# Two of eight final row tiles normalised by GpSimd and ScalarE in place of VectorE, in a hybrid encoder layer with a mixture of experts

## What is computed

```python
def expert_choice_moe(h, router_w, w_gate, w_up, w_down):      # tok: 512 tokens of one sequence
    gate, idx = lax.top_k(aff.T, cap)                           # cap = 64
    xs = tok[idx]
    hid = silu(xs @ w_gate) * (xs @ w_up)
    ye = (hid @ w_down) * gate[..., None]
    out = zeros_like(tok).at[idx].add(ye)

x = x + expert_choice_moe(rmsnorm(x, norm2_g), ...)
return rmsnorm(x, norm_f_g)                                     # the final norm, factor norm_f_g
```

## Time and profile before

| what | value |
|---|---|
| median of 3 runs | 1541.17 us |
| the profiled execution, its own time | 1543.18 us |
| its span, first to last instruction | 1541.4 us |
| mean granted TensorE clock | 0.977 of full |
| TensorE busy | 1464.4 us (95%) |
| VectorE busy | 1186.8 us (77%) |
| ScalarE busy | 816.1 us (53%) |
| GpSimd busy | 163.8 us (11%) |

### The profile page before, as it was taken

One profiled execution on the slowest core, in us unless ns is written; L12 is line 12 of the kernel. 1 busy time (PEld: TensorE's weight loads), 2 busy tenths in 40 slices (PEclk: granted clock), 3 DMA queues, 4 the chain that ended last, 5 costly groups with the idle time before them and its releaser, 6 DMA issues.

```text
span 1541.4 us, 18595 instructions
## 1 busy us (share of the span) xinstructions
PE 1464.4 (95%) x6886; PEld 1225.6 (80%) x6886; DVE 1186.8 (77%) x1002; ACT 816.1 (53%) x760; POOL 163.8 (11%) x121
## 2 busy tenths in 40 slices
PE   7999999999989999996499999999999999999994
PEld 6878888877768888785388888888888888888883
DVE  5688888985647766324698888888988888889887
ACT  5322332113621222323277777777777777777775
POOL 1000001000005200011101110111101111001110
PEclk9999999999989999998699999999999999999997
DMA  7110324422353245646899999999999999999995
GB/s 228 55 42 19 90 55 156 151 83 82 103 207 107 72 167 182 240 145 254 304 339 373 374 372 386 375 378 374 374 385 375 377 374 374 384 376 377 375 368 217
DMA packets 220745, 387.97 MB, mean 252 GB/s; under 512 B 8571, under 2 KB 87483, under 8 KB 220188
## 3 DMA queue, kind: packets, MB, share of 16 engines
q1 hardware_dynamic: 213468, 361.13, 65.9%
q0 software_dynamic: 7232, 26.22, 5.6%
HBM read 348.52 MB, written 38.80 MB: 251 GB/s over the span
## 4 chain that ended last, share of the span: by engine, by line
PE 49%; DVE 1%; DMA 0%; ACT 0%; issue 0%; POOLq 0%; POOL 0%
PE ps L1637 16%; PE ps L1639 15%; PE ps L1638 15%; PE ps L1965 1%; PE ps L1959 1%; DVE final_rows L1593 1%; DMA slot_tokens<-tok_rows,rows_to_gather 0%; DVE expert_lo L1130 0%; ACT expert_hi L782 0%; POOLq L83 0%; DVE expert_out L1604 0%; DVE expert_out L1611 0%; DVE slot_tokens_T_lo L1130 0%; ACT slot_tokens_T_hi L782 0%; ACT L1108 0%
## 5 line engine op out<-in xcount | busy, mean ns | idle before, releaser
L1130 DVE TENSOR_TENSOR expert_lo<-expert_raw,expert_hi 128x2048 fp32r<-128x2048 f32 (+1 forms) x288 | 604.2, 2112 | 94.4 <-ACT expert_hi L782 93.2
L782 ACT ACTIVATE expert_hi<-expert_raw 128x2048 fp32r<-128x2048 f32 (+1 forms) x288 | 511.3, 1777 | 182.9 <-PE ps L1639 179.2
L1637 PE MATMUL ps<-expert_hi,slot_tokens_T_hi 128*128 128x512 f32 (+1 forms) x768 | 290.6, 378 | 4.7 <-DVE slot_tokens_T_lo L1130 2.4
L1639 PE MATMUL ps<-expert_hi,slot_tokens_T_lo 128*128 128x512 f32 (+1 forms) x768 | 285.7, 372 | 0.0
L1638 PE MATMUL ps<-expert_lo,slot_tokens_T_hi 128*128 128x512 f32 (+1 forms) x768 | 285.6, 372 | 0.0
L1637 PE MATMUL ps<-hT_hi,w_hi 128*128 128x512 f32 x576 | 228.7, 397 | 0.6 <-DVE hT_lo L1142 0.6
L1639 PE MATMUL ps<-hT_hi,w_lo 128*128 128x512 f32 x576 | 225.3, 391 | 0.0
L1638 PE MATMUL ps<-hT_lo,w_hi 128*128 128x512 f32 x576 | 225.2, 391 | 0.0
L1637 PEld LDWEIGHTS ps<-expert_hi,slot_tokens_T_hi 128*128 128x128 f32 x768 | 144.5, 188 | 28.1 <-issue 3.8
L1639 PEld LDWEIGHTS ps<-expert_hi,slot_tokens_T_lo 128*128 128x128 f32 x768 | 144.6, 188 | 20.5
L1164 DVE SCALAR_TENSOR_TENSOR conv_sum<-a_padded,small_params,conv_sum 128x1024 f32<-128x1024 f32 x120 | 158.1, 1317 | 3.4
(11 more groups left out here) (269 smaller groups left out, 1839.3 us busy)
## 6 DMA issues: line engine op xcount, KB each, us to landing
expert_raw<-in_w_gate SPq DMA_DIRECT2D x64, 1024.0 KB, 9.0
expert_raw<-in_w_up SPq DMA_DIRECT2D x64, 1024.0 KB, 9.8
expert_raw<-in_w_down SPq DMA_DIRECT2D x64, 1024.0 KB, 8.1
expert_raw<-in_w_gate SPq DMA_DIRECT2D x32, 768.0 KB, 6.8
expert_raw<-in_w_up SPq DMA_DIRECT2D x32, 768.0 KB, 6.9
expert_raw<-in_w_down SPq DMA_DIRECT2D x32, 768.0 KB, 8.9
w_raw<-in_w_in SPq DMA_DIRECT2D x36, 512.0 KB, 4.8
gate_in<-gate_spill SPq DMA_DIRECT2D x22, 512.0 KB, 3.7
```

Source lines behind the costliest of these rows:

```text
L782: nc.scalar.activation(out, src, ACT.Copy, **scale).then_inc(s, 1)
L1130: V.tensor_tensor(out, src, high_part.bitcast(F32), ALU.subtract).then_inc(s, 1)
L1637: nc.tensor.matmul(out, a[0], b[0], start=first, stop=False)
L1639: return nc.tensor.matmul(out, a[1], b[0], start=False, stop=last)
```

## The change

Tiles 0 and 1 no longer pass through VectorE's product. GpSimd multiplies each by `NGF` in place as soon as ScalarE has taken its squares; later ScalarE scales it by the row's reciprocal root, in place. VectorE keeps the variance and the reciprocal of these two tiles. SP stores tiles 0 and 1 behind ScalarE's scaling.

```diff
+        EARLY_TILES = 2
...
             for t in range(TT):
-                sp.wait_ge(fin_out, t + 1)
+                if t < EARLY_TILES:
+                    sp.wait_ge(ln_root, 3 + t)
+                else:
+                    sp.wait_ge(fin_out, t + 1 - EARLY_TILES)
...
             nc.gpsimd.tensor_copy(DONE_ROWS[:], SLOTS[:, E - 1:E]).then_inc(rows_done, 1)
+            for t in range(EARLY_TILES):
+                pool.wait_ge(norm_g_in, 32)
+                pool.wait_ge(squares, TT + t + 1)
+                nc.gpsimd.tensor_tensor(XF[t][:], XF[t][:], NGF[:], ALU.mult).then_inc(tile_sum, 1)
...
+            def final_scale(t):
+                act.wait_ge(tile_sum, 4 + t)
+                act.wait_ge(square_sum, 2 + t)
+                nc.scalar.activation(XF[t][:], XF[t][:], ACT.Copy, scale=RSTDF[:, t:t + 1]).then_inc(ln_root, 1)
+
             final_root(0)
             final_root(1)
             for t, after in zip(FINAL_ORDER[2:], FINAL_ORDER[1:]):
                 final_square(t)
+                if t in (2, 3):
+                    final_scale(t - 2)
                 if t > 2:
                     final_root(after)
...
             def final_rows(t):
                 dve.wait_ge(roots, 2 * TT + FINAL_ORDER.index(t) + 1)
+                if t < EARLY_TILES:
+                    V.reciprocal(RSTDF[:, t:t + 1], RSTDF[:, t:t + 1]).then_inc(square_sum, 1)
+                    return
```

## The result

The changed kernel took 1548.63 us in the median of five runs (1544.81 to 1550.82), the kernel before 1541.17 beside it (five runs, 1539.79 to 1544.00). The ratio is 1.0038, with a 95% interval of [1.0023, 1.0054]: +5.9 us by the ratio (1541.17 x 0.0038). The prediction was 1546.5, +5.3 us, with a range up to 1548.5; the median lies 0.1 us above that range, and by the ratio the kernel takes 1547.0, inside it. The interval is wide: +3.5 to +8.3 us.

A forecast was written before the change was run, and what follows sets the result against it. The prediction took VectorE's tail from the second late addition on as the bound: gain 0, plus the later of ScalarE's +4.0 and TensorE's +5.3 us, on 1541.17 gives 1546.5 us; range 1542.2 to 1548.5.

The forecast's parts named there:

- Bound and gain: VectorE's tail from the second late addition on: removing two products saves only 0 to 0.2 us.
- Cost 1, the scalings: ScalarE: two scalings ahead of the square of tile 4 start the product of tile 2 1.7 us later (1.3 to 2.0).
- Cost 2, the turns: GpSimd's products hold VectorE's last two low parts: `hidden_T_lo` 3.0 us late, ScalarE's path +4.0 with the scalings.
- VectorE keeps the turn: Rival: VectorE's last low part isn't held by GpSimd's second product; end +1.8 or +3.7 us, chance 0.25.
- dearer half: Variance of tile 0 on VectorE waits for GpSimd's second product; end +3.7 us, half of that rival's 0.25.
- Cost 3, the clock: TensorE, idle 4.2 us, restarts its last 18 matmuls at half clock: 2.3 us more, second late half 5.3 late (4.6 to 6.5).
- is what the tail hangs on: The second late half, 5.3 us late by TensorE, sets the tail, being later than ScalarE's 4.0.
- The prediction's own sign for this: VectorE waiting for ScalarE's square ahead of the variance of tile 4 would show the scalings lead, not TensorE; no size given.

The follow-up runs named there:

- late_products: The changed kernel with GpSimd's two products waiting for their tile's variance, so that they start behind `hidden_T_lo`; ratio 1.0013, tail 35.34 us.
- second_later: turns_both with a small GpSimd fill (128x256) ahead of the product of tile 1, which then came 0.27 us later; tail 34.51 us.
- turns_both: The kernel before plus GpSimd's products of tiles 0 and 1 into spare tiles, VectorE keeping all eight products, no scalings; ratio 1.0044, tail 38.38 us.
- turn_second: The kernel before plus GpSimd's product of tile 1 alone, into a spare tile; tail 33.32 us.
- after_again: The changed kernel executed once more, nothing altered; tail 38.97 us against 38.63 at first.
- keep_busy: The changed kernel plus 17 matmuls into an unused bank ahead of TensorE's last 18; tail 37.13 us.
- scales_last: The changed kernel with both ScalarE scalings behind the last square and tiles 0 and 1 stored late; ratio 1.0062, tail 39.60 us.
- one_tile: The changed kernel with only tile 0 moved, GpSimd's product and ScalarE's scaling later, VectorE's product of tile 2 ahead of the second late half; ratio 0.9996, tail 32.46 us.
- turn_first: The kernel before plus GpSimd's product of tile 0 alone, into a spare tile; tail 35.69 us.

## Why the prediction was right, and where it was not

**Bound and gain: right.** The tail was VectorE's from the second late addition on, and taking two products off it gave, in this order of its list, only VectorE's 0.2 us of lateness behind the last matmul. In after the second late half starts 0.04 us after the last matmul's end, in before 0.19 us.

**Cost 1, the scalings: right when alone** (+1.7 forecast, +2.0 in late_products, 0.65 of them waits for GpSimd). The price of one was below the 1.15 taken: the next activation starts 1.04 to 1.06 us later.

**Cost 2, the turns: right** in both, with the order and the lengths (3.50 and 3.89 where "some 3.5" and "about 4" stood) and `hidden_T_lo` +3.06 for +3.0. The margin of 0.1 to 0.2 us was 0.12, and second_later shows that it decides: the rival "VectorE keeps the turn" is what turns_both becomes when GpSimd's product comes a quarter of a microsecond later. Its dearer half, the +3.7 by a held variance, fell: 128x1 operations ran beside GpSimd's product in turn_second at 0.20 us for two.

The Trainium skill ("SBUF — State Buffer", "Who interferes with whom") says that whoever issues first has the shared ports for the whole instruction and the other blocks fully, and that the order of issue decides who blocks. The prediction read in it no order for two that both wait; taken as the order of issue for them too, its rule agrees with the traces, by 0.12 us either way (after, second_later). The section also names tensor_scalar, which the prediction took as speaking for the +3.7; at 128x1 none waited (turn_second).

**Cost 3, the clock: the mechanism right, the size not the same in every execution.** "I take 5 us, 12 matmuls, 2.3 us" was nine matmuls and +1.6 in the profiled execution of after, the lower of the two bounds; it was eleven and +2.2 in turns_both, and twelve and +2.4 in after_again. In after TensorE's path is then 3.05 + 1.60 = 4.65 us later at its last matmul and 4.5 at the second late half, for a forecast 5.3; in after_again that half is the forecast 5.3 late.

**The step that failed: "is what the tail hangs on".** The prediction took ScalarE's path as +4.0 and TensorE's as a separate one. They are joined. The reciprocal of tile 1 stands in VectorE's list behind the first late half, and the second scaling waits for it; so TensorE's half clock reaches ScalarE. From the rows of after: root 0 is 2.3 us late, the first scaling adds 1.04, the wait for the reciprocal 1.71, the second scaling 1.06; that is 6.1, less the 0.6 of slack and 0.2 of small gaps that ScalarE had before: +5.3 at the variance of tile 4. The prediction's own sign for this, VectorE waiting for the square ahead of that variance, is in the profile with 0.71 us. That the sum of +5.3 came out to the tenth is luck: 0.8 too much on TensorE's path stood against 1.3 too little on ScalarE's. In after_again, where TensorE's term was as forecast, the product of tile 2 is 5.6 us late, again by ScalarE. Without the clock's fall ScalarE's path is +3.8 (keep_busy), near its +4.0.

**How the parts add.** The turns alone make +5.07 and the scalings alone +2.0, together +5.3: each hides in the other's waiting. (With after's nine matmuls at the lower clock in place of eleven the turns alone would be about +4.5, an estimate from the two traces.) Undoing the scalings alone would win little (scales_last: the product of tile 2 only 0.8 earlier), undoing the turns 3.3 us (38.63 - 35.34).

**The range.** Its upper end allowed for the tail and for 0.8 us of spread between medians. The spread is larger, which the three times shown hid: medians of the kernel before were 1541.17, 1542.49 and 1543.6 in three sets of runs. Its lower end, 1542.2, is 0.2 us below what its own terms give (1541.17 + 1.7 - 0.5 = 1542.4).

## What to carry to other kernels

Before work is moved to GpSimd, look in VectorE's timeline for the next operations with two SBUF inputs whose results TensorE waits for, and place the work behind them; two held operations of 1.76 us became an idle TensorE and a lower clock, and a wait on another semaphore removed it. Ask of each operation added to an engine what it waits for in the other engines' lists, since a 0.15 us reciprocal behind a late addition joined two paths here that had been separate. And count what a freed engine can win only up to the next thing it waits for: of 2.6 us taken off VectorE 0.2 were to be had with its list left in order; one_tile's 0.85 came from a later product put into the gap.

## What the runs showed of the hardware

**The order of two engines that wait is that of arrival, to about 0.1 us.** 0.12 us ahead, GpSimd went first (after; 0.10 in turns_both); 0.12 us ahead, VectorE did (second_later). A held low part loses its wait less some 0.15 us: 3.89 - 1.76 = 2.13 lost, for a wait from 1512.76 to the end of GpSimd's product at 1515.04, 2.28.

**The same idle time lowered TensorE's clock once and once not.** After 2.09 us of it the granted clock was 0.53 over the next 3.6 us (turn_first), after 2.10 us it was 1.00 (second_later). What decides it isn't settled: the two kernels differ in the turns, and there is one trace of each.

**Half clock in mid-kernel is most of the scatter.** The same program text far ahead of the change ran at different clocks. Busy time from 425 to 435 us, first in before, then in late_products:

```profile
425.00:430.00 5.00, 4.79 (x16) 4.13 (x17) 5.00 (x6) 3.94 (x5) 0.00 (x0) 0.56 0.16 63
430.00:435.00 5.00, 5.00 (x19) 4.01 (x18) 3.24 (x7) 0.00 (x0) 0.00 (x0) 0.76 0.02 3
```

```profile
425.00:430.00 5.00, 5.00 (x24) 4.13 (x23) 5.00 (x5) 1.82 (x2) 0.00 (x0) 1.00 0.01 3
430.00:435.00 5.00, 5.00 (x24) 4.14 (x23) 1.11 (x5) 0.00 (x0) 0.00 (x0) 1.00 0.00 0
```

Before is at 0.56 and 0.76 here, late_products at 1.00 (after 0.66 and 1.00, after_again 0.55 and 0.77). Before has 35 matmuls in ten microseconds and late_products 48, 13 x 0.21 = 2.7 us at their pace, and the tail of late_products begins 4.8 us earlier. After against before, by the clocks 5 x (0.10 + 0.24) = 1.7 us at full speed lie in this stretch, of the 3.6 us by which its tail began earlier. That an experiment's edit behind this stretch changes its clock is not likely, as after and after_again differ as well.

All 14 traces say the same. For each, TensorE's busy time up to 1500 us, in steps of 10 us, times what the clock lacked of full speed gives the time lost to it: from 8.0 us in late_products, whose tail begins at 1503.26, to 12.2 in one_tile, at 1508.34, all of it between 400 and 800 us. Loss and start of the tail go together (correlation 0.86, 1.1 us per us), within 1.5 us either way. So do the times: four runs of the kernel before with a mean granted clock of 0.979 have a median of 1540.3 us, sixteen with 0.976 one of 1544.0. No experiment set this clock, so what is shown is that the two go together; the rest of the scatter is not explained.
